# Second attention of a two-layer decoder: the softmax shift turned by one transposition and moved by two transfers

## What is computed

```python
    q_nope, q_pe = q[..., :B_NOPE], q[..., B_NOPE:]
    k_nope, v = kv[..., :B_NOPE], kv[..., B_NOPE:]
...
    def attend_block(args):
        qn, qp, b = args
        q_pos = N_META + b * BLOCK + jnp.arange(BLOCK)
        s = (jnp.einsum('bqhd,bshd->bhqs', qn, k_nope)
             + jnp.einsum('bqhd,bsd->bhqs', qp, k_pe)).astype(jnp.float32)
        s = jnp.where(k_pos[None, :] <= q_pos[:, None], s, NEG_INF)
        p = jax.nn.softmax(s, axis=-1).astype(v.dtype)
        return jnp.einsum('bhqs,bshd->bqhd', p, v)
```

## Time and profile before

| | |
|---|---|
| median of 3 runs | 3559.33 us |
| lowest and highest | 3557.93 and 3562.45 us |
| profiled execution, its time | 3558.93 us |
| its span | 3557.1 us |
| TensorE busy over the span | 3198.7 us (90%) |
| GpSimd, VectorE, ScalarE busy | 1791.8, 1765.5, 1249.4 us |
| granted TensorE clock, mean | 0.949 |

### The profile page before, as it was taken

How to read it: one execution, slowest core, us unless ns; L and a number is a source line. 1 busy time by engine, 2 the same in 40 slices (tenths; PEclk the granted TensorE clock), 3 DMA queues, 4 the chain that set the end, 5 groups by cost and what they waited for, 6 DMA issues and landing times. The chain is left out here.

```text
span 3557.1 us, 57727 instructions
## 1 busy us (share of the span) xinstructions
PE 3198.7 (90%) x20065; PEld 2492.4 (70%) x20065; DVE 1765.5 (50%) x3672; ACT 1249.4 (35%) x2673; POOL 1791.8 (50%) x1443
## 2 busy tenths in 40 slices
PE   6999998997999995997999999999998987999950
PEld 4788886785888884996566666666656876888840
DVE  3555555676343333664554554555534663433316
ACT  2444444232223222443443444444343222232212
POOL 2555554343344431444689778877872223444312
PEclk9999999998999997998899999999999998999975
DMA  2010102642999975886320221021005439999817
GB/s 100 26 39 26 39 33 74 194 153 92 369 317 306 304 244 171 254 266 173 67 51 7 51 54 48 10 51 51 7 13 188 145 113 318 360 313 312 292 66 325
DMA packets 357633, 535.63 MB, mean 151 GB/s; under 512 B 81873, under 2 KB 277749, under 8 KB 350532
## 3 DMA queue, kind: packets, MB, share of 16 engines
q1 hardware_dynamic: 330468, 456.94, 40.1%
q0 software_dynamic: 26976, 76.27, 5.6%
HBM read 396.93 MB, written 144.92 MB: 152 GB/s over the span
## 5 line engine op out<-in xcount | busy, mean ns | idle before, releaser
L2074 POOL TENSOR_TENSOR ab_acc<-ab_acc,ab_pT 128x1024 f32<-128x1024 f32 (+2 forms) x320 | 593.5, 1855 | 129.0 <-ACT ab_pT L2108 96.4
L2108 ACT ACTIVATE ab_pT<-ab_S 128x512 f32<-128x512 f32 (+4 forms) x704 | 352.5, 504 | 560.3 <-PE ab_S L2185 301.2
L2124 DVE TENSOR_REDUCE ab_mx<-ab_W 128x2 f32<-128x1024 f32 (+5 forms) x352 | 346.4, 994 | 377.7 <-PE ab_W L2200 252.1
L1264 POOL DMA_INDIRECT scratch_y<-ex_y,ex_prow x64 | 64.8, 1012 | 491.9 <-issue 353.0
L1434 PE MATMUL ex_G<-ex_xT,ex_wg 128*128 128x160 f32 x2048 | 293.3, 302 | 2.7 <-DMA ex_wu<-in_moe_w_up 2.7
L1434 PE MATMUL ex_U<-ex_xT,ex_wu 128*128 128x160 f32 x2048 | 288.6, 299 | 0.0
L2183 PE MATMUL ab_S<-ab_q_hi,ab_k_hi 97*128 97x512 f32 (+4 forms) x704 | 279.6, 397 | 9.5 <-ACT ab_pT L2108 8.3
L1434 PEld LDWEIGHTS ex_G<-ex_xT,ex_wg 128*128 128x128 f32 x2048 | 281.6, 191 | 7.8 <-issue 3.6
L2234 PE MATMUL ab_O<-ab_pT,ab_v 128*64 128x512 f32 (+4 forms) x1408 | 283.9, 519 | 0.0
L1434 PEld LDWEIGHTS ex_U<-ex_xT,ex_wu 128*128 128x128 f32 x2048 | 281.7, 190 | 0.0
L2184 PE MATMUL ab_S<-ab_q_lo,ab_k_hi 96*128 96x512 f32 (+4 forms) x704 | 249.9, 355 | 0.0
(11 more groups left out here) (308 smaller groups left out, 7041.4 us busy)
## 6 DMA issues: line engine op xcount, KB each, us to landing
ex_wg<-in_moe_w_gate SPq DMA_DIRECT2D x64, 1024.0 KB, 7.0
ex_wu<-in_moe_w_up SPq DMA_DIRECT2D x64, 1024.0 KB, 10.7
ex_wd<-in_moe_w_down SPq DMA_DIRECT2D x64, 1024.0 KB, 11.8
pb_y<-scratch_y SPq DMA_DIRECT2D x17, 1024.0 KB, 6.8
pr_o<-scratch_oT SPq DMA_DIRECT2D x33, 512.0 KB, 4.7
scratch_h<-pr_h SPq DMA_DIRECT2D x33, 512.0 KB, 5.0
scratch_xn<-pr_xn SPq DMA_DIRECT2D x33, 512.0 KB, 2.7
fi_y<-scratch_y SPq DMA_DIRECT2D x16, 1024.0 KB, 14.0
```

The costliest lines, as they stand in the source:

```text
L2074: nc.gpsimd.tensor_tensor(to, to, pT[0:r, U % RING, :, 0:n], ALU.add).then_inc(added, 1)
L2108: nc.scalar.activation(pT[0:r, U % RING, h, 0:n], S[0:r, h, 0:n], ACT.Exp, scale=B_SCALE).then_inc(exped, 1)
L2124: nc.vector.reduce_max(mx[:, :, t, c:c + 1].rearrange("p h a -> p (h a)"), W[:, j % 2, :, 0:n], AX.X).then_inc(emptied, 1)
```

## The change

One instruction of TensorE now turns all columns of the group. `m` becomes a 128 x 128 tile, zeroed once, in which group `g` has its eight columns at 32 g to 32 g + 7. `shift` on TensorE transposes the whole tile once (L2221 of the new kernel), so that the eight maxima rows stand on partitions 32 g to 32 g + 7 of the slot of `W`; VectorE negates these 8 x 128 elements into a new tile `turned` (L2146), and SyncE, at the shift's place in the order of units, waits for that and issues two transfers, one per head, that carry four rows of 128 into the 512 elements of `q_hi`'s row 96 (L2045). TensorE waits for their landing (`shifted[g]`, 32 per shift) where it waited for VectorE.

```diff
-        m = s.sb("m", [P, 2, NT])
+        m = s.sb("m", [P, P])
+        turned = s.sb("turned", [P, P], F32R)
...
+                        if kind == "shift":
+                            g = at[0]
+                            sp.wait_ge(m_turned, shift_count[p, g])
+                            for h in range(2):
+                                sp.dma_start(q_hi[QD:QD + 1, p % 2, h, P * (4 * g + 1):P * (4 * g + 5)].bitcast(F32),
+                                             turned[32 * g + 4 * h:32 * g + 4 * h + 4, :].bitcast(F32)).then_inc(shifted[g], 16)
                         if kind == "divide":
...
+                nc.gpsimd.memset(m[:, :], 0.0)
...
-                        last = nc.vector.reduce_max(m[:, h, t0:t1], mx[:, h, t0:t1, 0:g + 2], AX.X)
+                        last = nc.vector.reduce_max(m[:, 32 * g + 4 * h:32 * g + 4 * h + 4], mx[:, h, t0:t1, 0:g + 2], AX.X)
...
                 def shift(j, p, g):
                     dve.wait_ge(filled, j + 1)
-                    cols = slice(P * (4 * g + 1), P * (4 * g + 5))
-                    nc.vector.tensor_scalar(q_hi[QD:QD + 1, p % 2, :, cols], W[QD:QD + 1, j % 2, :, :], -1.0, None, ALU.mult).then_inc(shifted, 1)
+                    if NG * p + g >= NG:
+                        dve.wait_ge(shifted[g], 32 * p)
+                    nc.vector.tensor_scalar(turned[32 * g:32 * g + 8, :], W[32 * g:32 * g + 8, j % 2, 0, 0:P], -1.0, None, ALU.mult).then_inc(m_turned, 1)
                     dve.drain().then_inc(emptied, 1)
...
-                        pe.wait_ge(shifted, shift_count[p, g])
+                        pe.wait_ge(shifted[g], 32 * (p + 1))
...
                 def shift(j, p, g):
                     pe.wait_ge(m_ready, NG * p + g + 1)
                     room(j)
-                    for h in range(2):
-                        for k in range(4):
-                            one = m[:, h, 4 * g + 1 + k:4 * g + 2 + k]
-                            last = nc.tensor.transpose(W[:, j % 2, h, P * k:P * k + P], one.to_broadcast([P, P]), ident[:, :])
-                    last.then_inc(filled, 1)
+                    nc.tensor.transpose(W[:, j % 2, 0, 0:P], m[:, :], ident[:, :]).then_inc(filled, 1)
```

More of the change, by code:

```diff
@@ L1965, in attention_b @@
         m_ready = s.sem("m_ready")
-        shifted = s.sem("shifted")
+        m_turned = s.sem("m_turned")
+        shifted = s.sems("shifted", NG)
         scored = s.sem("scored")
```

## The result

| | before | changed |
|---|---|---|
| median | 3559.36 us | 3564.95 us |
| lowest and highest | 3551.06 and 3564.26 us | 3559.68 and 3569.81 us |
| number of runs | 22 | 22 |
| profiled execution, time (span) | 3558.93 (3557.1) us | 3568.21 (3566.4) us |

The ratio is 1.0015, with a 95% interval from 1.0008 to 1.0021: 5.3 us more (5.6 between the medians), clear of no change at all, but within the 0.2% of "same". 3561 had been forecast. The small difference is the rest of two large terms: a stall of 25 us at the start of the stage, and as much saved on TensorE behind it.

A forecast was written before the change was run, and what follows sets the result against it. TensorE was taken as the bound; −21.6 (transpositions) −1.1 (slot wait) +0.5 (second opening) +25.1 (stall) −1.0 (clock) = +1.9 us, from the median of 3559.33 to 3561 us. Range of 8 in 10: 3550 to 3570.

The forecast's parts named there:

- The balance: Whole stage: one stall of 25 us against 30 savings of 0.7 us, nearly even; 59 in 100.
- Stall at (0,0): First group's opening: transfers issued behind SyncE's loads in a full queue land late, 25.1 us more, between 23.6 and 25.8.
- The rival in which small transfers do not queue: First opening: transfers land 2 us after issue, opening +8.6 instead of +25.1 us, total 3546 us; 8 in 100.
- The one transposition: TensorE, each shift: the one that stays costs 0.12 us where eight took 0.80; 21.6 us less over 30 shifts.
- VectorE's slot wait: Behind shift (0,2): TensorE's wait for the slot that VectorE's negation frees goes, 1.1 us less.
- (0,1): Second group, one unit of cover: 3.4 us from transposition to opening instead of 2.96, 0.5 us more.
- The clock: Behind the first opening: 10.9 us at half clock instead of 12.9, 1.0 us less.
- the falls of the clock move: Pairs' starts: new timing redraws the falls; none gives 3554 or 3551 us, three more 3571; faster side 14 in 100.
- The fourth groups: Tightest steady groups, four units: 7.7 us left from transposition to opening, so the transfers are covered.
- GpSimd did not become the bound: Rival: GpSimd takes over when TensorE gets shorter, so the change does less; small, inside the range, no chance of its own.
- The loss of some 3 us per pair: Second attention: a pair loses only some 3 us of its 120, said in the rival of another engine taking over.

The follow-up runs named there:

- the later raising: ScalarE prepares the next pair's queries and keys from unit 6, not 4; changed kernel with (0,0) the old way: 3529.03 us, with (0,1) the old way too: 3523.96 us.
- the pair of kernels without the stall: The changed kernel with shift (0,0) alone done the old way, 3539.96 us, and with (0,0) and (0,1) both the old way, 3541.56 us.

## Why the prediction was right, and where it was not

**The balance** was the forecast, and it came: +24.8 of stall against −23.7 of work, by the trace +1.1 before the clock. That the sum came within 4 us is in part luck: the work was 1.5 us below the forecast and the clock some 5 above it. Step by step:

- *Stall at (0,0)*: 25.1 forecast, 24.8 measured; from the first scan to the opening it is 34.0 us in this profile and 34.7, 32.5 and 32.2 in the three others that keep the stall, that is 23.0 to 25.5 above the 9.17 of before. The mechanism, transfers behind loads in a full queue, is shown from both sides: another queue cuts the wait to 5.1 us, ten loads fewer ahead to 8.8. The rival in which small transfers do not queue had 3546, with the opening 8.6 us late. In the changed kernel they did queue. The kernel with ScalarE as issuer comes to 3545.93, but by another sum: its opening is only 2.9 us late, and 47.6 us of its stage ran at half clock. That the two numbers agree is chance.
- *The one transposition* was mis-sized: 0.12 us taken, 0.03 to 0.08 measured in the stream (0.13 and 0.21 at the first and the last shift). For 30 shifts that is 1 to 3 us more saved than the 21.6 forecast. VectorE's slot wait went, as forecast.
- *(0,1)*: 0.5 us more forecast, nothing measured in the changed kernel, since the empty queue took 2.33 us from the negation's end to TensorE's start, where 2.8 had been reckoned. That the queue is surely empty there is owed to the stall at (0,0): in the four profiles with a short stall or none the wait was 1.7, 1.8, 1.8 and 3.8 us. This coupling was not seen.
- *The clock* is the term that failed: −1.0 us forecast. Its first part held, since half clock behind the opening lasted 11.7 us, where 10.9 had been taken. (One row was misread on the way: from the matmul at 2694.09 to the rise at 2697.7 are 3.6 us, not 4 to 5.) But the prediction looked at that opening only. With 22 runs at +5.3 us and +1.1 from stall and work, some 4 us are left, and the half clock of all runs gives 3.8. In the profiled execution they are falls of the clock elsewhere: 17.1 us of half clock behind the second opening, and 17.0 later, where 17.0 us in all had been; with the 1.2 us less behind the first opening that is 15.8 us more (7.9 us of time). The rival "the falls of the clock move" had this as a matter of luck in both directions; on the average of the runs it had a sign. Why is open in part: TensorE's waits at the pairs' starts are as long as before (7.6 us against 8.3), but a fall came with two of the six before and with two to five in each of the eight profiles of changed kernels that keep these waits.
- *The fourth groups*, 7.7 us of cover forecast, had 7.64 to 7.67 us from transposition to opening and no wait. GpSimd did not become the bound, though it now holds TensorE once, for 1.0 us. The loss of some 3 us per pair that the prediction names is in no row: TensorE idles 0.7 us of 100 in the earlier trace rows.

**What stays open** is how much of those 4 us is the wait at (0,1). With the later raising it costs 5.1 us (a wait of 3.8 us in the profile), with the stall 4 to 6 at the edge of the noise, and in the pair of kernels without the stall (a wait of 1.8 us) nothing that could be measured. Half clock between the second opening and that of group 3 was 3.4, 13.7 (four times), 16.6 and 23.9 us in the profiles with transfers at (0,1), and 0, 0, 3.4, 3.4, 10.2 and 10.2 in those without. And in all seven with transfers a fall began within 1.5 us of the second opening, in the six others none within 18 us of it. So the wait brings this fall, but a fall that does not come here often comes later, and each profile shows one execution.

## What to carry to other kernels

A transfer that moves a few kilobytes inside the core costs nothing where units of work lie between its issue and its use, and costs the whole rest of the queue where it stands behind bulk loads: look at the tightest place, at the start of the stage above all, and keep the direct way there or issue it from an engine whose queue is empty. Keeping the old way for the first shift alone turned +5 us into −21. When TensorE is the bound, count its waits of one to two microseconds at more than their length (1.6 times here), since the clock may fall with them. And since one profile's falls are partly chance, compare the granted clock of all runs before explaining a few microseconds by it.

## What the runs showed of the hardware

- Two transfers of 2 KB in a queue of their own took 5.4 us from the first issue to TensorE's start with the DMA engines fully busy; behind loads in the same queue they took 19.6, and 2.3 to 2.5 us at the second opening in the six profiles in which that queue was empty.
- Within this stage, behind the first rise, the clock fell 47 times in the thirteen profiles, each time between 1.3 us before and 2.0 us behind the end of a wait of TensorE of 0.4 to 3.8 us. Where ScalarE's waits at the pairs' starts are gone, the falls there are gone too, but for one with a wait for GpSimd. In the kernel with only (0,1) the old way four falls of 3.4 us began at 2108.9, 2228.3, 2347.8 and 2467.3, at the starts of four pairs in a row, each 0.3 to 1.7 us behind a wait of 1.3 to 1.9 us for ScalarE. The first of them (timeline, then clock):

```profile
2107.19 0.50 PE L2211 MATMUL ab_S<-ab_q_hi,ab_k_hi 97*128 97x512 f32 x1 [1.75 <-ACT ab_pT L2127]
```

```profile
2108.90:2112.30 3.40, 3.40 (x10) 2.71 (x9) 1.28 (x2) 2.43 (x6) 2.38 (x1) 0.50 0.01 1
2112.30:2120.00 7.70, 7.70 (x36) 3.73 (x37) 4.51 (x3) 4.85 (x9) 4.75 (x2) 1.00 0.01 2
```

- Not every such wait is followed by a fall: at 2214.3 in the kernel before, 1.94 us of waiting left the clock at 1.00 until 2225.
- Eight transpositions in a row step by 0.10 us, one alone in a stream of matmuls by 0.03 to 0.08, at a record of 0.27.
